# Modulation rows of a three-block network: asked for and read in other places

## The reference, cut to what matters

```
mod = jax.nn.silu(c) @ w_ada[l] + b_ada[l]
sh1, sc1, g1, sh2, sc2, g2 = jnp.split(mod[:, None, :], 6, axis=-1)
h = rms_norm(x, norm_g[l, 0]) * (1.0 + sc1) + sh1
...
x = x + g1 * mix
h = rms_norm(x, norm_g[l, 1]) * (1.0 + sc2) + sh2
x = x + g2 * conv_ffn(h, w_up[l], conv_w[l], conv_b[l], w_down[l])
```

## Time and profile before

| | |
|---|---|
| median of 3 runs | 2523.4 us (2522.47 to 2524.72) |
| the profiled execution | 2524.96 us, its span 2523.2 us |
| TensorE busy | 2434.6 us (96%) |
| VectorE busy | 1624.6 us (64%) |
| ScalarE busy | 848.0 us (34%) |
| GpSimd busy | 281.4 us (11%) |
| chain that ended last | TensorE 84%, transfers 7%, VectorE 5% |
| reads of modulation rows | 192, two groups with a mean of 1228 and 1241 ns |

### The profile page before, as it was taken

The page is one execution under the profiler, slowest core; times in us unless marked ns, Lnnn a source line. Parts: engine busy times, 40 slices in busy tenths (PEclk is TensorE's granted clock), DMA queues, the critical chain, the costliest instruction groups (busy, mean ns, idle before and its releaser), DMA issues.

```text
span 2523.2 us, 45753 instructions
## 1 busy us (share of the span) xinstructions
PE 2434.6 (96%) x17188; PEld 2288.6 (91%) x17188; DVE 1624.6 (64%) x3772; ACT 848.0 (34%) x2205; POOL 281.4 (11%) x374
## 2 busy tenths in 40 slices
PE   5989999999999999999999999999999999999999
PEld 4878889888888878999999999988889999999998
DVE  6686664664664653695887884334629958888634
ACT  2542120344211112222665550022532246655300
POOL 0020110001010001011111111100300101111211
PEclk8999999999999999999999999999999999999999
DMA  9328888422887853499999999964037989999997
GB/s 368 111 101 305 301 287 318 164 74 80 308 305 282 301 214 101 144 414 378 375 403 384 406 407 414 392 234 132 18 101 273 415 330 407 407 375 415 405 415 297
DMA packets 172064, 729.14 MB, mean 289 GB/s; under 512 B 19216, under 2 KB 19728, under 8 KB 146960
## 3 DMA queue, kind: packets, MB, share of 16 engines
q1 hardware_dynamic: 143568, 523.86, 55.7%
q0 software_dynamic: 27648, 201.34, 19.7%
q10 hardware_dynamic: 704, 2.10, 0.4%
HBM read 724.07 MB, written 1.05 MB: 287 GB/s over the span
## 4 chain that ended last, share of the span: by engine, by line
PE 84%; DMA 7%; DVE 5%; ACT 2%; issue 2%; SPq 0%; DVEq 0%; ACTq 0%
PE banks L732 36%; PE lev L1101 22%; PE banks L1047 20%; DMA ring<-in_peer_u 3%; DMA extra<-in_ada 3%; PE lev L732 2%; DMA arena<-in_ada 1%; DVE arena L1748 1%; PE lev L1028 1%; PE banks L1028 1%; ACT arena L1361 0%; ACT arena L1335 0%; PE lev L873 0%; DVE arena L1832 0%; DVE arena L1968 0%
## 5 line engine op out<-in xcount | busy, mean ns | idle before, releaser
L732 PE MATMUL banks<-hT,ring 128*128 128x256 f32 (+1 forms) x3024 | 631.9, 370 | 22.6 <-ACT hT L1279 22.4
L732 PEld LDWEIGHTS banks<-hT,ring 128*128 128x128 f32 x3024 | 554.0, 192 | 97.5 <-issue 21.7
L1047 PE MATMUL banks<-hT,ring 128*128 128x160 f32 x4096 | 579.7, 301 | 3.0 <-DMA ring<-in_peer_u 3.0
L1101 PE MATMUL lev<-arena,ring 128*128 x4096 | 576.5, 301 | 0.0
L1047 PEld LDWEIGHTS banks<-hT,ring 128*128 128x128 f32 x4096 | 559.2, 190 | 5.1 <-issue 2.1
L1101 PEld LDWEIGHTS lev<-arena,ring 128*128 128x128 f32 x4096 | 558.9, 190 | 0.0
L1719 POOL DMA_INDIRECT arena<-in_peer_rows,keysb x192 | 184.0, 958 | 1139.0 <-DVE consts L2126 681.5
L732 PE MATMUL banks<-arena,ring 128*128 128x256 f32 (+2 forms) x1648 | 284.7, 334 | 5.5 <-issue 4.2
L732 PEld LDWEIGHTS banks<-arena,ring 128*128 128x128 f32 x1648 | 258.7, 192 | 30.3 <-issue 4.6
L2173 DVE SCALAR_TENSOR_TENSOR extra<-consts,chT 128x192 bf16<-128x192 f32 x640 | 223.7, 408 | 17.8 <-ACT arena L1408 17.7
L2138 DVE CUSTOM_DVE_ANT_0 arena<-arena 128x1024 f32<-128x1024 f32 x64 | 78.2, 1221 | 166.3 <-DMA arena<-in_peer_rows,keysb 166.3
(11 more groups left out here) (280 smaller groups left out, 2296.4 us busy)
## 6 DMA issues: line engine op xcount, KB each, us to landing
ring<-in_peer_u SPq DMA_DIRECT2D x256, 512.0 KB
ring<-in_peer_v SPq DMA_DIRECT2D x256, 512.0 KB
ring<-in_stream_first SPq DMA_DIRECT2D x192, 512.0 KB
arena<-in_ada SPq DMA_DIRECT2D x104, 512.0 KB, 5.5
extra<-in_ada SPq DMA_DIRECT2D x88, 512.0 KB, 5.3
ring<-in_stream_nsa SPq DMA_DIRECT2D x45, 512.0 KB
ring<-in_stream_fox SPq DMA_DIRECT2D x41, 512.0 KB
arena<-in_peer_rows,keysb POOLq DMA_INDIRECT x192
```

What stands on the lines that cost most here:

```text
L732: ins = nc.tensor.matmul(o, lhsT, rhs, start=start, stop=stop, **kw)
L1047: ins = nc.tensor.matmul(banks[k // 2 % 4][:, (k % 2) * ND:(k % 2 + 1) * ND], ring[:, u % RING, c], hT[:, c, NS:T], start=c == 0, stop=c = ...
L1101: ins = nc.tensor.matmul(lev[c // 4][:, (c % 4) * T + NS:(c % 4 + 1) * T], ring[:, u % RING, c], a[:, bass.ds(g, 1), k], start=False, stop ...
```

## The change

It moves requests for modulation rows on SyncE and reads of them on VectorE; no instruction of TensorE, ScalarE or GpSimd moves, and the number of rows is the same.

1. Layer 0: the 20 rows that were all asked for behind unit 27 are asked for as 14 behind unit 27 and 6 behind unit 29. VectorE reads them where it did.
2. Layer 1: the last six steps of the up-projection read three rows in place of two, and the additions of the down-projection have 6, 6, 6 rows before them in place of 8, 8, 8.
3. Both layers: the three runs of rows in the down-projection are asked for three units earlier (behind units 52, 57, 62 counted from the start of the up-projection, instead of 55, 60, 65).
4. Third mixer: the last 16 rows are asked for behind units 24 to 31 in place of 7 to 14, and VectorE reads two before each of the 8 attention units in place of all 16 before the mixer's work. `mods(3, 0, 6)` moves from there into the third mixer's `residual`, between the third addition and the first half tile's.

```diff
-        ADA_TURNS = [[24] + [2] * FC + [8, 8, 8, 0], [0] + [2] * FC + [8, 8, 8, 0]]
+        ADA_TURNS = [[24] + [2] * FC + [8, 8, 8, 0], [0] + [2] * 16 + [3] * 6 + [6, 6, 6, 0]]
...
-        ADA_FOX = EARLY - 16 - sum(map(sum, ADA_TURNS))
+        assert EARLY - 16 - sum(map(sum, ADA_TURNS)) == 16
...
-                    if k == U_IN + 5:
-                        load_ada(ADA_TURNS[l][0] - ADA_LEVELS[l])
+                    if l == 0 and k in (U_IN + 5, U_IN + 7):
+                        load_ada(14 if k == U_IN + 5 else ADA_TURNS[0][0] - ADA_LEVELS[0] - 14)
                     at = k - (U_IN + U_OUT)
                     if at >= 6 and at % 2 == 0 and at < U_UP + 6:
                         load_ada(next(turns))
-                    elif at >= U_UP + 10 and (at - U_UP) % 5 == 1:
+                    elif at - U_UP in (8, 13, 18):
                         load_ada(next(turns))
...
                 load_unit(io["stream_fox"][k], B_FOX + k)
-                if k >= RING - 1:
+                if k >= U_FOX - DC - 1:
                     load_ada(2)
...
-            do_ada(ADA_FOX)
-            mods(3, 0, 6)
             seq(V.memset(vF, 0.0), "vF_zero")
...
-            attention(("attF",), fox_units(), F0)
-            residual(5, ("foxout",), 2, 2)
+            attention(("attF",), fox_units(), F0, [2] * 8)
+            do_ada(EARLY)
+            residual(5, ("foxout",), 2, 2, late=lambda: mods(3, 0, 6))
```

## The result

The changed kernel takes 2527.07 us (median of 20 runs, 2522.47 to 2531.87); the kernel before took 2523.59 (median of 20 beside it, 2520.9 to 2526.74). The ratio is 1.0015 with an interval of 1.0009 to 1.0021, so 2.3 to 5.3 us slower. The profiled execution took 2527.44 us, its span 2525.6, against 2524.96 and 2523.2.

What follows compares the result with a forecast made beforehand. TensorE, busy for 96% of the span, was taken as the bound. Gains of 14.8 us less costs of 14.15 us gave a net gain of 0.65 us and 2522.7 us, with an 8 in 10 range of 2517 to 2529.5.

Steps and rivals of the forecast that it cites:

- the sum's first term: Layer 0's output projection: splitting the row requests removes the wait for unit 28, a gain of 4.3 us, bounds 2.9 and 5.5.
- I take 1.25, since its reads were paced about equally by both: Layer 0's third addition on VectorE: 1.25 us later, between 0 with slack and 2.6 if transfers alone set the pace.
- The lower bound of this term, 2.9: Layer 0's output projection: smallest gain expected from the split, 2.9 us.
- The down-projections: Ends of the down-projections: the 2.13 us wait in layer 1 goes, gaining 2.1 us, and 0.1 in layer 0.
- Three reads a step: Last six up-projection steps of layer 1: VectorE still waits about 1 us a step, cost 0, at most 1 us.
- The third mixer's start: Statistics and projections before the third mixer's attention: two waits and the lower clock go, gaining 8.3 us, lower bound 5.0.
- The attention: Third mixer's attention: 16 reads make VectorE the pace, costing 12.75 us, plus 0.6 for transfers and 0.8 for the clock.
- the 4.5 us that the forecast named as a sign of being wrong: Third mixer's attention: a step over 4.5 us, from transfers or GpSimd, would show the prediction wrong.
- The 0.8 us for the clock: Third mixer's attention: cost of 0.8 us, between 0 and 2, for TensorE's clock after pauses near 2.5 us.
- The third (the waits come back, 2526.2 us): Rival: the four waits move and return, gains only 11.4 us, 2526.2 us; counted within the 0.70 for no change.
- The second (faster): Rival: gains at upper bounds, attention at its lower, 2519.4 us, or 2516.4 with 3 us more from the tail; chance 0.13.
- The first rested on GpSimd: Rival, third mixer's attention: GpSimd multiplications delay VectorE's second reads, 5.8 us over seven units, 2528.5 us; chance 0.17.

Runs made afterwards that it cites:

- early_only: Kernel before with one edit: layer 0's 20 rows asked for as ten behind unit 28 and ten behind unit 29; 2516.85 us, ratio 0.9976.
- threes: Changed kernel with layer 0's rows ten behind unit 28, ten behind 29, three rows in all 22 layer 1 up-projection steps, none in the third mixer; 2508.07 us.
- turns_only: Kernel before with only the up- and down-projection rows moved (three a step in layer 1's last six, 6, 6, 6, requests three units earlier); 2523.18 us, ratio 0.9999.
- one_each: Changed kernel with one row, not two, per third-mixer attention unit, the eight others moved to layer 1 up-projection steps; 2516.21 us, ratio 0.9967.
- reads_only: Changed kernel without the requests for the last 16 rows and the waits for them, reads kept; 2528.04 us, ratio 1.0012.
- fox_only: Kernel before with the third mixer's edits alone (last 16 rows read two ahead of each attention unit, `mods` late); 2530.12 us, ratio 1.0025.
- early_units: Changed kernel with layer 0's 20 rows asked for as ten behind unit 28 and ten behind unit 29; 2524.15 us, ratio 1.0006.
- split_only: Kernel before with only layer 0's row requests split, 14 behind unit 27 and 6 behind unit 29; 2519.65 us, and 2521.77 us when run again.
- threes_split: `threes` with layer 0's output projection rows asked for as in the changed kernel, 14 and 6; 2511.22 us.

## Why the prediction was wrong, by its own steps

The time, 2527.07 us, lies inside the range of 2517 to 2529.5, but the forecast was a gain of 0.65 us and the kernel became 3.5 us slower.

**The step that failed is the sum's first term, the output projection of layer 0: 4.3 us forecast, none in the traced pair, 0.8 us between the means of the traces.** It was right that the wait for unit 28 goes, and that the half tile then ends early: TensorE turned to the statistics at 204.56 us, and 205.8 less the 1.09 is 204.7. It was wrong in "I take 1.25, since its reads were paced about equally by both", for the lateness of the third addition. The end of 2.6 us, "if transfers had been the only pace", was the true one: VectorE stood 2.89 us for row 34 and the addition was 2.9 us late. The reads had a slack only so long as the rows ahead were already there. Both units stand behind a row that waits for VectorE, so they go out together as soon as it may be asked for, and the rows behind them land later by the time of both.

The other half was not priced at all: with a wait of 3 us there the clock is as low (0.66 from 206 to 212 us) as with the one of 4.18 (0.73). Against `early_only`, where nothing waits, the changed kernel's stretch is 5.6 us longer. 3.0 of it are the wait. Then from the first of the four statistics matmuls behind the wait to the x12 row the traces have 7.45 us (208.64 to 216.09) where `threes` at a clock of 1.00 has 4.57 (207.53 to 212.10), so 2.9 are the clock, 0.59 in this stretch (the two make 5.9; the modelled ends overlap by some 0.1, and 16 matmuls behind them are 0.2 shorter here). The forecast had a lower clock behind this wait in none of its cases. The lower bound of this term, 2.9, took the late addition without the clock: with it the bound would have been 0. One thing speaks for the forecast: by its medians the split alone gained 4.3 and 2.0 us, which the traces of this stage don't explain.

**The down-projections: not shown, and the second step that failed.** 2.43 and 0.44 in the traced pair against 2.1 and 0.1 look right, but that is luck. The forecast took a wait of one execution for one of the kernel: the wait of the earlier trace rows is gone in every trace with the new turns, and in the four others with the old ones as well. The means give 0.5 us, and `turns_only` took 0.8 us less with an interval of -2.5 to +2.0.

**Three reads a step: right, and with room for more.** The rest fell from 2.33 to 1.07 us, as worked out from the earlier trace rows, and `threes` put three in each of the 22 steps for nothing.

**The third mixer's start: right.** 8.13 against 8.3, with both waits and the low clock of 911 to 920 gone (0.73 there before, 1.00 now). Five traces with the old start have 81.2 to 83.1 us there, mean 82.3, and all eight with no reads there 73.2, so the gain is 8 to 10 us.

**The attention: right within 0.5 us, and by its mechanism.** Forecast 14.15, found 14.67. The first reading of scores to the last took 30.8 us where 29.0 were forecast. The first reads of the eight units stand 3.20, 3.66, 3.81, 3.86, 3.84, 4.15 and 4.79 us apart where 3.65 was worked out for a step; the difference is mostly 1.9 us of waits for rows at three units (forecast 0.6), and the last step is over the 4.5 us that the forecast named as a sign of being wrong. The 0.8 us for the clock were not needed: the last read of scores ends 5.0 us ahead of the output projection in both kernels, so the low clock (0.81 from 960 to 975 us) stayed hidden behind VectorE. That the whole came within 0.5 us is in part these two cancelling. `one_each` shows the bend that the working assumed (8.3 us of VectorE's work in 16.3, the rest free): its 2.3 us lie where 8 x 1.27 + 8.3 - 16.25 = 2.2 puts them. `reads_only` gives the transfers 1.1 to 1.6 us.

**The sum once more, from means.** Take each stage as the difference of the means of all traces that have its one form or the other: -0.8 for the output projection of layer 0, -0.6 for the down-projections, -9.1 for the third mixer's start, +14.75 for 16 reads in its attention. That is +4.2 us for the changed kernel, where its two medians say +3.5 and +4.1; for `fox_only` it is +5.6 (measured +6.2), for `threes` -15.2 (-15.8), for `early_units` -0.4 (+0.3). It misses by more where only layer 0's rows moved: `early_only` -5.5 (-7.1), `split_only` -0.8 (-4.3 and -2.0), and `threes_split` -10.5 (-12.5). Against the forecast the first term lacks 3.5 us and the second 1.6.

**The rivals.** The third (the waits come back, 2526.2 us) named what happened in layer 0, a half tile that waits 2.6 us for a late addition, with 3.03 found; it also had the third mixer's statistics wait, which they did not, so that its 2526.2 lies near the measured time in part by luck. The second (faster) hoped for something in the tail behind the last read, and the tail kept its 5.0 us. The first rested on GpSimd and VectorE getting in each other's way. They do, but GpSimd loses by it (1.89 us for a pair in place of 0.93) and VectorE hardly (1.26 and 1.36 us for the second read of two in place of 1.22). Two of GpSimd's pairs in the changed kernel's attention, the reads beside the second, and the reads as groups (busy, mean ns, idle before):

```profile
959.38 2.71 POOL L1696 TENSOR_SCALAR arena<-arena,rinv 128x128 f32<-128x128 f32 x2 [175.25 <-DVE rinv L1842]
962.82 1.89 POOL L1696 TENSOR_SCALAR arena<-arena,rinv 128x256 f32<-128x256 f32 x2 [0.73 <-DVE rinv L1842]
```

```profile
959.31 1.22 DVE L1748 CUSTOM_DVE_ANT_0 arena<-arena 128x1024 f32<-128x1024 f32 x1
...
960.58 1.26 DVE L1748 CUSTOM_DVE_ANT_0 arena<-arena 128x1024 f32<-128x1024 f32 x1
...
964.42 1.36 DVE L1748 CUSTOM_DVE_ANT_0 arena<-extra,arena 128x1024 f32<-128x1024 f32 x1
```

```profile
L1748 DVE CUSTOM_DVE_ANT_0 arena<-extra,arena 128x1024 f32<-128x1024 f32 x8 | 10.1, 1262 | 2.1 <-DMA extra<-in_ada 1.9
L1748 DVE CUSTOM_DVE_ANT_0 arena<-arena 128x1024 f32<-128x1024 f32 x8 | 9.9, 1238 | 7.8 <-ACT arena L1572 7.5
```

The first pair, of a size that took 0.72 us in the kernel before, begins 0.07 us behind a read and lasts until both reads are through. Windows of 0.02 us put the end of its first multiplication at 960.76, 0.23 us behind the end of the first read: so GpSimd does get one in as the reads change, as the rival said, but the read beside it is longer by 0.04 us (0.14 at the next pair) and not by a whole multiplication. Of the pairs, the second takes 1.89 in place of 0.93. The sixteen reads took 20.0 us together where 16 x 1.226 are 19.6. So the multiplications beside them cost VectorE, which is the pace, 0.4 us in all and not 5.8. In this trace the two multiplications of the first pair, 0.36 us each in the kernel before, end 0.23 and 0.25 us behind the end of a read (960.76 behind 960.53, 962.09 behind 961.84): it is GpSimd that stands while a read runs. (The profile's spans on GpSimd are rough.)

## What to carry to other kernels

When a request is moved ahead of others in one queue, take the whole transfer time of what goes ahead as the lateness of what comes behind (here 2.6 us for two units at 401 GB/s, and an addition 2.9 us late), unless the consumer is seen waiting for something else just then; and place it where the queue is empty, not where it is merely allowed (ten and ten against 14 and 6: same bytes, 3.8 to 5.8 us shorter in the stretch, 2.8 to 3.15 in the medians). A wait that was cut from 4.2 to 3.0 us kept its price in the clock (0.73, then 0.66, from 206 to 212 us), so price what is left of a wait together with the matmuls behind it. Before a wait goes into a sum, look whether a second trace has it: the 2.13 us of the earlier trace rows were in one of five. VectorE, 46% busy in the attention before, took reads there for little until it was full, then at full price: 8 cost 2.3 us, 16 cost 14.7. So spread such work over stretches with room (22 steps with 1 us of rest each took it all).

## What the runs showed of the hardware

TensorE's granted clock (1.00 is full) behind one wait at the same place, over ten traces: with waits of 0, 0.56 and 1.44 us it stayed at 1.00; with 2.41, 2.73, 3.03, 3.27, 3.32, 3.61 and 3.63 us the next 16 matmuls took 3.00 to 3.62 us in place of 1.95. The clock fell to 0.50 of full in both traces of the changed kernel (208 to 214 us). In the third mixer's attention the clock fell behind a wait of 2.31 us (959.13; 0.50 from 959 to 962) and was back at 1.00 before the output projection (from 974 on), while at 855 in the kernel before it stayed at 1.00 (855 to 857) behind a wait of 2.13 us. The length of the one wait doesn't decide it in these traces: later in the same attention a wait of 3.29 us was followed by a clock of 1.00,

```profile
984.24 0.71 PE L732 MATMUL banks<-arena 128*128 128x128 f32 x4 [3.29 <-ACT arena L1372]
```

```profile
980.00:990.00 10.00, 6.47 (x48) 5.83 (x47) 5.18 (x16) 4.31 (x10) 1.65 (x4) 1.00 0.04 6
```

and the wait at the same place was followed by a clock of 0.50 in `fox_only` (2.78 us; 987.5 to 989.5) and by 1.00 in the changed kernel's second trace (2.77; 983 to 987).

In layer 0's output projection a row asked for with no unit ahead of it was there after 5.0 us at most in the kernel before; with two units of 524 KB ahead, at 416 GB/s, it took 7.9 us in the changed kernel's first trace and 8.7 in its second.
